# Expert stage of a hybrid encoder step: from 128 gathered and 416 dense tokens to 160 gathered and 384 dense

## The chip, the cores and the metric

One core of a Trainium2 chip (trn2) runs the whole step. The metric is the device time of one execution in microseconds. Engines are named as in the profile: PE (TensorE matmul), PEld (its weight loads), DVE (VectorE), ACT (ScalarE), POOL (GpSimd), SP (SyncE, which here only issues DMAs).

## The reference, cut to what matters

544 tokens (512 of a prompt, 32 of a running stream) pass an input projection, stick-breaking attention, an RWKV-7 branch, a mixing and an output projection, and then the expert layer, which is what the change touches:

```python
q = (xf @ w_q).reshape(n, PEER_HEADS, 2, PEER_HALF)
...
best, sel = lax.top_k(cand, PEER_TOPK)
idx = jnp.take_along_axis(cidx, sel, axis=-1).reshape(n, PEER_HEADS * PEER_TOPK)
gate = jax.nn.softmax(best, axis=-1).reshape(n, PEER_HEADS * PEER_TOPK).astype(xn.dtype)
...
u = jnp.take(u_tab, ib, axis=0)
h = jax.nn.gelu(jnp.einsum('nkd,nd->nk', u, xb), approximate=False)
vv = jnp.take(v_tab, ib, axis=0)
return jnp.einsum('nk,nkd->nd', gb * h, vv)
```

Each token picks 8 x 16 = 128 of 16,384 experts. An expert has a row of 2048 floats in u_tab and one in v_tab. The output is the sum of the 128 rows of v, each times gate times gelu(row of u . token). All is float32.

## The kernel before, in words

**Two ways for the expert layer.** For the first TD = 416 tokens the layer is computed densely: all 16,384 experts are multiplied with all tokens, and a matrix of gates, zero except for a token's picks, selects. For the last 128 tokens only the picked rows are fetched: one indirect DMA on POOL's queue (L2016) brings, for pick number s, one row of 8 KB per partition (128 tokens on 128 partitions, so 1 MB), first 128 times from u (turned by the program into rows in u_d beforehand), then 128 times from v. DVE takes the dot product of a u row with its token (L2251, the token in PSUM, the four banks of accs) and adds a v row times its coefficient to Y (L2259, R and Y both in SBUF). R has GBUF = 3 buffers; a gather waits until its buffer has been used.

**Units.** The dense work is made of weight units of 128 x 2048 floats (1 MB) in a double buffer (class Stream, L119). SP loads a unit into raw (L145), ACT rounds it to whi (L150 whole, L164 half), POOL computes wlo = raw - whi (L154, L168), PE multiplies in three terms (product, L227): whi x hi, whi x lo, wlo x hi, so 16 blocks x 3 = 48 matmuls per unit with all TD tokens as columns. A unit of u is 128 experts by all 2048 channels. A unit of v is 256 experts by 1024 channels (v_rows, L242): for each of 8 blocks of 128 channels PE makes 6 matmuls into one PSUM bank, and DVE adds the bank to H (L2241). So there are 128 units of each, 12,288 matmuls with 416 columns, and 1,024 additions to H. Units of the projections instead make 96 matmuls with 272 columns.

**Where the u units run.** 2 run in the second norm, 24 in retrieval (the choice of the picks, L1522), 16 in gate_matrix (L1775) and 2 at the start of experts (L1886); their gelu is stored in pre_d. Retrieval has 8 iterations, one per head, in which DVE finds the picks. gate_matrix has 8 blocks of GB_T = 52 tokens; in each, PE makes 13 groups ("quads") of one-hot products between matmuls of the units, ACT copies them to STG and SP stores them to g_d.

**experts.** FIRST = 22 groups of 256 experts have their u part already; for these only v units run, with H's additions from four banks of accs. chi and clo, the high and low parts of the coefficients (gelu x gate, made by DVE L2224, ACT L2138, DVE L2230), have two slots, so that those of the next group are made while PE multiplies this one. Then the tokens of the gathered part are turned into rows (32 small matmuls, L2093 and L2094, ACT L2185, L2189). In the 42 groups after that two u units (into psS) and two v units (into psR and psS) alternate, and the 256 gathered rows are spread over them by hand: phases (L1914) says how many gathers POOL issues and between which halves of wlo, and rows_of (L2243) where DVE takes the rows between its additions. Each engine runs its own list in order; the semaphores ex_added, ex_coef, gx_done and those of Stream tie them together. At the end Y is turned back (L2110) and added to H, and the last norm runs.

Of the kernel before, what the change touches and what calls it, by code (L numbers as in the profile page):

```python
# [14 lines left out]
P = 128  # L15
# [18 lines left out]
TD = 416  # L34
# [18 lines left out]
GBUF = 3  # L53
# [65 lines left out]
class Stream:  # L119
# [37 lines left out]
    def half(self, t, c, h):  # L157
        return t[:, c % 2, :].rearrange("p (k e n) -> p k e n", k=2, e=2)[:, :, h, :]
# [81 lines left out]
def v_rows(A):  # L240

    return A["v"].rearrange("(g k p) (h n) -> g h p k n", k=2, p=P, h=2)  # L242


def build(nc, A, O):
    ctx = ExitStack()
    with ctx:
# [35 lines left out]
        with ExitStack() as back:  # L283
            sbk = lambda n, s, d=F32: back.enter_context(nc.sbuf_tensor(n, s, d))

            hh, hl = sbk("hh", [P, KB, T], F32R), sbk("hl", [P, KB, T], F32R)
            load_h = lambda a, b: h_d[a:b].rearrange("k p t -> p k t")
# [12 lines left out]
            IDX, GT = sbk("IDX", [P, P], U32), sbk("GT", [P, P])  # L300
            with ExitStack() as picks:
                IT = picks.enter_context(nc.sbuf_tensor("IT", [P, 3, TD], F32))
                iota = picks.enter_context(nc.sbuf_tensor("iota", [P, P], F32))
                retrieval(nc, S, A, W.phase(base["retrieval"]), [A["u"][TAIL], A["u"][TAIL + 1]], acc, psS, psR, hh, hl, IT, iota, IDX, GT, pre_d)
                gate_matrix(nc, S, A, W.phase(base["gates"]), [A["u"][PRE - 2], A["u"][PRE - 1]], acc, psS, psR, hh, hl, IT, iota, g_d, pre_d)
            H = sbk("H", [P, KB, T])
            experts(nc, S, A, W.phase(base["experts"]), accs, psS, psR, H, load_h, hh, hl, IDX, GT, g_d, pre_d, u_d)
# [1214 lines left out]
def retrieval(nc, S, A, W, ahead, acc, psS, psR, hh, hl, IT, iota, IDX, GT, pre_d):  # L1522
# [4 lines left out]
    with ExitStack() as ctx:  # L1527
# [11 lines left out]
        GEL = sb("tk_GEL", [P, 2, TD])  # L1539
        N = 4  # L1540
        OFF = [0, P, 2 * P, TD, 3 * P]
# [9 lines left out]
        def _(sp):  # L1551
# [27 lines left out]
            blocks(AFTER // 2 - 1, True)  # L1579
            for u in range(2):  # L1580
                sp.wait_ge(S[f"tk_kept{u}"], 16 * (TAIL // 2))

# [11 lines left out]
        def _(pe):  # L1594
# [31 lines left out]
            for j, t in enumerate((0, 1, 2, 4)):  # L1626
# [8 lines left out]
        def _(act):  # L1635
# [37 lines left out]
            for j, t in enumerate((0, 1, 2, 4)):  # L1673
# [6 lines left out]
        def _(dve):  # L1680
# [79 lines left out]
            picked = lambda a: OUT[:, a, 3].rearrange("p h k -> p (h k)")  # L1760
            dve.scalar_tensor_tensor(IDX[:, :], picked(0), float(NK), picked(1), ALU.mult, ALU.add)
            dve.wait_ge(S["tk_gate"], 4)
            dve.tensor_copy(GT[:, :], picked(2)).then_inc(S["tk_gather"], 1)
            dve.wait_ge(S["tk_gather"], 1)


GB_T = 52
# [7 lines left out]
def gate_matrix(nc, S, A, W, ahead, acc, psS, psR, hh, hl, IT, iota, g_d, pre_d):  # L1775
# [3 lines left out]
    with ExitStack() as ctx:  # L1779
# [5 lines left out]
        STEPS = [2, 2, 3, 2, 3, 2, 3, 2, 3, 2, 3, 2, 3]  # L1785
        ITER = GB_N // 2
        MIDDLE = QUADS // 2
        SLOT = [*range(4)] * 3 + [1]
# [97 lines left out]
def experts(nc, S, A, W, accs, psS, psR, H, load_h, hh, hl, IDX, GT, g_d, pre_d, u_d):  # L1886


    with ExitStack() as ctx:
        sb = lambda n, s, d=F32: ctx.enter_context(nc.sbuf_tensor(n, s, d))  # L1890
        G = sb("Ge", [P, 2, GB_N, 2, GB_T])
        GE = sb("GE", [P, 2, TD])
        chi, clo = sb("chi", [P, 2, 2, TD], F32R), sb("clo", [P, 2, 2, TD], F32R)
        R, Y = sb("R", [P, GBUF, D]), sb("Y", [P, D])
        HD, identr = sb("HD", [P, P]), sb("identr", [P, P], F32R)
        GROUPS = NK // 2
        N = 8
        even, odd = R[:, 0, 0:T], R[:, 0, D // 2:D // 2 + T]
        squares = [R[:, 1, 0:T], R[:, 1, D // 2:D // 2 + T], R[:, 2, 512:512 + T], R[:, 2, 1280:1280 + T]]
        square_at = lambda d: (even, odd)[d] if d < 2 else squares[(d - 2) % 4]  # L1900
        all_ones = R[:, 2, 0:P]
        v_units = v_rows(A)
        block = ctx.enter_context(nc.Block())
        FIRST = PRE // 2
        ITER = (GROUPS - FIRST) // 2 - 1
        C0 = START + 2 * FIRST
        UNITS = C0 + 2 + N * ITER + 6

        u_bank = lambda c: psS[:, c % 2, 0:TD]
        v_banks = [psR[:, 0, 0:TD], psR[:, 1, 0:TD], psS[:, 0, 0:TD]]  # L1910
        v_bank = lambda d, per: v_banks[d % 3] if per == N else accs[:, d % 4, 0:TD]
        early = R[:, 2, 0:2 * TD].rearrange("p (k t) -> p k t", k=2)

        gathers, phases = [], []  # L1914
        dotted = summed = 0
        for j in range(GROUPS - FIRST):
            in_u, in_v = 4, 2 + j % 4 // 3 if j else 0
            nv = min(dotted - summed, 3 if dotted < P else in_u + in_v)
            nu = min(in_u + in_v - nv, P - dotted)
            us, vs = [("u", dotted + n) for n in range(nu)], [("v", summed + n) for n in range(nv)]  # L1920
            order = us[:1] + vs + us[1:]
            phases.append((order[:in_u], order[in_u:], len(gathers)))
            gathers += order
            dotted, summed = dotted + nu, summed + nv
        assert dotted == P and summed == P, (dotted, summed)
# [7 lines left out]
        def _(sp):  # L1933
            def u_unit(c, i, k):
                W.load(sp, row(A["u"], k), c, N, i)

            def v_unit(c, i, group, half, per=N):
                src = v_units[group, half] if isinstance(group, int) else v_units[bass.ds(group, 1), half].rearrange("g p k n -> (g p) k n")
                W.load(sp, src, c, per, i)

            def gates(group, slot, count):
                sp.wait_ge(S["ex_coef"], count)
                src = g_d.rearrange("b p n t -> p b n t")
                if isinstance(group, int):
                    a = src[:, :, 2 * group:2 * group + 2, :]
                else:
                    a = src[:, :, bass.ds(2 * group, 2), :]
# [8 lines left out]
            for h in range(2):  # L1956
                v_unit(2 + h, 0, 0, h)
# [415 lines left out]
```

## Time and profile before

| | |
|---|---|
| Median of 3 runs | 4850.69 us (4841.92 to 4850.75) |
| The profiled execution | 4852.76 us, its span 4850.9 us |
| PE busy | 4605.5 us (95%) |
| POOL busy | 2246.2 us (46%) |
| DVE busy | 2973.9 us (61%) |
| Mean granted TensorE clock | 0.98 |
| gate_matrix, experts | from about 2563 us, from about 2825 us to the end |

Matmuls are pipelined: a matmul of 0.35 us begins while the one before it is still counted, so the distance between two starts is what a matmul costs, not its duration. A line at L236 is the helper product, so stages are told apart by the tiles. Spans on POOL are rough. Windows of the stretch from 3400 to 4700 us lie inside the 42 groups.

### The profile page before, as it was taken

How to read it: one execution, taken by the hardware profiler on the slowest of the kernel's cores; microseconds unless marked ns; L12 is line 12 of the kernel's file. 1: busy time of each engine (PE TensorE's matmuls, PEld its weight loads, DVE VectorE, ACT ScalarE, POOL GpSimd, SP SyncE). 2: the span in 40 equal slices, each digit the busy share in tenths (PEclk: the TensorE clock that was granted, in tenths of full speed). 3: DMA queues.
4: the chain of work that ended last, by engine and by line, in shares of the span. 5: the costliest groups of instructions: out<-in, count | busy, mean ns of one | idle time of the engine just before them, and what ended most of it. 6: DMA issues, size and time to landing. Idle time of an engine off the chain costs nothing. (4 is left out here: it accounts for less than half of the span.)

```text
span 4850.9 us, 88014 instructions
## 1 busy us (share of the span) xinstructions
PE 4605.5 (95%) x33924; PEld 4418.6 (91%) x33924; DVE 2973.9 (61%) x4755; ACT 1398.0 (29%) x1813; POOL 2246.2 (46%) x865
## 2 busy tenths in 40 slices
PE   6999899999999898979999989999999999999997
PEld 5999888888888798979998989999999999999997
DVE  4333355555555432259977946657777777777777
ACT  3333322222222221122223323333332333233332
POOL 1332221222222232334443245547787777778876
PEclk8999999999999999999999999999999999999999
DMA  6999733334443477942233465448888888888884
GB/s 237 345 367 359 284 129 133 122 127 134 134 134 133 154 221 267 313 148 95 104 124 150 182 248 161 158 148 305 296 304 307 304 292 303 310 299 297 307 292 170
DMA packets 344256, 1078.68 MB, mean 222 GB/s; under 512 B 99457, under 2 KB 154113, under 8 KB 264961
## 3 DMA queue, kind: packets, MB, share of 16 engines
q1 hardware_dynamic: 292272, 784.66, 46.7%
q0 software_dynamic: 36864, 268.45, 14.8%
q10 hardware_dynamic: 14928, 22.84, 1.3%
q8 instruction: 142, 2.33, 0.2%
q14 instruction: 50, 0.40, 0.0%
HBM read 877.69 MB, written 198.14 MB: 222 GB/s over the span
## 5 line engine op out<-in xcount | busy, mean ns | idle before, releaser
L154 POOL TENSOR_TENSOR wlo<-raw,whi 128x2048 fp32r<-128x2048 f32 x174 | 803.1, 4616 | 2020.7 <-ACT whi L150 1725.2
L168 POOL TENSOR_TENSOR wlo<-raw,whi 128x1024 fp32r<-128x1024 f32 x424 | 1040.6, 2455 | 498.9 <-ACT whi L164 492.2
L164 ACT ACTIVATE whi<-raw 128x1024 fp32r<-128x1024 f32 x424 | 449.7, 1061 | 983.9 <-PE psR L236 367.0
L236 PE MATMUL accs<-xh,whi 128*128 128x272 f32 x2624 | 581.8, 303 | 56.0 <-POOL wlo L154 26.6
L2259 DVE SCALAR_TENSOR_TENSOR Y<-R,HD,Y 128x2048 f32<-128x2048 f32 x127 | 441.4, 3476 | 233.6 <-DMA R<-in_v,IDX 229.2
L236 PE MATMUL accs<-xh,wlo 128*128 128x272 f32 x2624 | 547.5, 290 | 0.0
L236 PE MATMUL accs<-xl,whi 128*128 128x272 f32 x2624 | 546.5, 290 | 0.0
L236 PE MATMUL accs<-hh,whi 128*128 128x272 f32 (+1 forms) x1696 | 465.3, 323 | 47.2 <-POOL wlo L154 22.4
L236 PEld LDWEIGHTS accs<-xh,whi 128*128 128x128 f32 x2624 | 416.8, 190 | 86.0 <-issue 39.4
L236 PE MATMUL psS<-hh,wlo 128*128 128x416 f32 x1344 | 474.1, 353 | 0.0
L236 PE MATMUL psS<-hh,whi 128*128 128x416 f32 x1344 | 471.0, 350 | 0.0
L236 PE MATMUL psS<-hl,whi 128*128 128x416 f32 x1344 | 469.3, 349 | 0.0
L236 PE MATMUL accs<-hh,wlo 128*128 128x272 f32 (+1 forms) x1696 | 451.2, 315 | 0.0
L236 PE MATMUL accs<-hl,whi 128*128 128x272 f32 (+1 forms) x1696 | 449.4, 314 | 0.0
L236 PEld LDWEIGHTS accs<-xl,whi 128*128 128x128 f32 x2624 | 417.2, 191 | 0.0
L236 PEld LDWEIGHTS accs<-xh,wlo 128*128 128x128 f32 x2624 | 415.4, 191 | 0.0
L150 ACT ACTIVATE whi<-raw 128x2048 fp32r<-128x2048 f32 x174 | 332.4, 1911 | 142.1 <-DMA raw<-in_w_out 73.1
L236 PEld LDWEIGHTS accs<-hh,whi 128*128 128x128 f32 x1696 | 291.2, 190 | 58.8 <-POOL wlo L154 24.4
L210 DVE STREAM_TRANSPOSE at_UO<-at_UI 128x2048 f32<-128x2048 f32 x64 | 147.9, 2312 | 310.2 <-DMA at_UI<-in_u 310.0
L236 PE MATMUL psR<-chi,whi 128*128 128x416 f32 x924 | 330.2, 357 | 0.7 <-DVE H L2241 0.5
L236 PE MATMUL psR<-chi,wlo 128*128 128x416 f32 x924 | 326.1, 353 | 0.0
L236 PE MATMUL psR<-clo,whi 128*128 128x416 f32 x924 | 323.7, 350 | 0.0
(406 smaller groups left out, 9313.0 us busy)
## 6 DMA issues: line engine op xcount, KB each, us to landing
raw<-in_u SPq DMA_DIRECT2D x128, 1024.0 KB, 4.9
raw<-in_v SPq DMA_DIRECT2D x128, 1024.0 KB, 5.7
raw<-in_w_in SPq DMA_DIRECT2D x82, 1024.0 KB, 8.5
at_UI<-in_u SPq DMA_DIRECT2D x64, 1024.0 KB, 9.2
u_d<-at_UO SPq DMA_DIRECT2D x256, 256.0 KB, 6.5
g_d<-STG SPq DMA_DIRECT2D x8, 3328.0 KB, 10.3
Ge<-g_d SPq DMA_DIRECT2D x64, 416.0 KB, 10.8
wo_UI<-in_u SPq DMA_DIRECT2D x24, 1024.0 KB, 8.4
```

The costliest lines, as they stand in the source:

```text
L150: act.activation(self.hi[:, c % 2, :], self.raw[:, c % 2, :], ACT.Copy).then_inc(self.hi_done, 2)
L154: pool.tensor_tensor(self.lo[:, c % 2, :], self.raw[:, c % 2, :], self.hi[:, c % 2, :].bitcast(F32), ALU.subtract).then_inc(self.split_don ...
L164: act.activation(self.half(self.hi, c, h), self.half(self.raw, c, h), ACT.Copy).then_inc(self.hi_done, 1)
L168: pool.tensor_tensor(self.half(self.lo, c, h), self.half(self.raw, c, h), self.half(self.hi, c, h).bitcast(F32), ALU.subtract).then_inc(se ...
L210: dve.transpose(self.uo(b).rearrange("p (e k j) -> p e k j", e=4, j=32), self.ui(a).rearrange("p (k e j) -> p e k j", e=4, j=32)).then_inc ...
L236: mm = pe.matmul(out, w(k), x(k, n), start=a, stop=z)
L2259: dve.scalar_tensor_tensor(Y[:, :], r, HD[:, x:x + 1], Y[:, :], ALU.mult, ALU.add).then_inc(S["gx_done"], 1)
```

## The change

The dense part takes TD = 384 tokens and 160 are gathered. The last 128 tokens ("A") are gathered as before. The 32 others ("B") are laid out four picks at a time: partition 32r + t holds pick 32r + n of token t, so 32 gathers bring all their 128 rows of each table. That makes 160 gathers from u and 160 from v. The picks of B are moved to their partitions by 8 small DMAs at the end of retrieval; their tokens are turned by 32 more small matmuls at the start of experts and stand in SBUF (XB), where those of A still stand in PSUM (accs). The sums of B's four partitions per token are made at the end by 16 matmuls with sel. YA, YB and XB lie in columns of H, hh and hl that the dense part doesn't use any more.

A unit of v now holds 512 experts by 512 channels: 4 blocks of 128 channels with 12 matmuls each, so still 128 units with 48 matmuls, but 512 additions to H instead of 1,024. A row of v in a unit is read in pieces of 2 KB instead of 4 KB. Groups have 512 experts: FIRST = 11 without u units, then 21 with four u units and four v units. chi and clo have one slot for the four key blocks instead of two for two. The v units use the four banks psR and psS in turn, and accs is kept for the tokens of A from the start. Gathers run in the first phase too (2 in group 0, 4 in each of the next ten), 13 or 14 in each of the twenty groups after that, 7 in the last, with four buffers. POOL issues a gather by a written time table (when, issue). gate_matrix has GB_T = 48, 12 quads per block.

```diff
-TD = 416
+TD = 384
...
-GBUF = 3
+GBUF = 4
...
-    return A["v"].rearrange("(g k p) (h n) -> g h p k n", k=2, p=P, h=2)
+    return A["v"].rearrange("(g k p) (h n) -> g h p k n", k=4, p=P, h=4)
...
+                sp.dma_start(IDXB[part, :], IB[:, cols]).then_inc(S["few_moved"], 16)
+                sp.dma_start(GTB[part, :], OUT[0:DEC, 2, 4].rearrange("p h k -> p (h k)")[:, cols]).then_inc(S["few_moved"], 16)
...
-GB_T = 52
+GB_T = 48
...
+        G, GE = sb("Ge", [P, GB_N, 4, GB_T]), sb("GE", [P, 4, TD])
+        CHI, CLO = sb("chi", [P, 4, TD], F32R), sb("clo", [P, 3, TD], F32R)
...
+        YA, YB, XB = H[:, :, spare], over[0][:, :, spare], over[1][:, :, spare]
...
+        chi = lambda k: CHI[:, k, :]
+        clo = lambda k: CLO[:, k, :] if k < 3 else hh[:, 0:TD // DEC, tail]
...
+        SUPERS, FIRST, U = NK // 4, PRE // 4, 8
...
+        u_bank = lambda n: psS[:, n % 2, 0:TD]
+        v_bank = lambda dd: (psR, psS)[dd // 2][:, dd % 2, 0:TD]
...
+        seq = [x for n in range(DEC) for x in [("A", 4 * n + m) for m in range(4)] + [("B", n)]]
...
+                  "long": [(0, 0.1), (0, 0.4), (0, 0.7), (1, 0.3), (1, 0.7), (2, 0.3), (2, 0.7), (3, 0.3),
+                           (4, 0.4), (5, 0.1), (5, 0.8), (6, 0.2), (6, 0.8), (7, 0.2)]}
...
+        issue = [max(3.0, when[n - GBUF] + 0.4 if n >= GBUF else 0.0) for n in range(len(gathers))]
...
+            def first_groups(i, begin):
+                for h in range(begin, 4):
+                    v_unit(START + h, i, i, h, 4)
+                sp.wait_ge(S["ex_prod"], 4 * i + 4)
+                gates(i + 1)
+                for k in range(4):
+                    sp.wait_ge(S["ex_coef"], 4 * i + k + 1)
+                    kept(i + 1, k)
...
+            for c in range(2, UNITS):
+                for h in range(2):
+                    gather(c - 1.4 + 0.5 * h)
...
+            def v_first(c, i, s, per):
+                for half in range(2):
+                    W.ready(pe, c, per, i, half)
+                for k in range(4):
+                    pe.wait_ge(S["ex_coef"], 4 * s + (k + 1 if per == 4 else max(k + 1, 3)))
+                    for dd in range(3):
+                        if k == 0:
+                            pe.wait_ge(S["ex_added"], 16 * s + dd + 1)
+                            if per == 4:
+                                pe.wait_ge(S["ex_xb_read"], dd + 1)
+                        mm = channel(c, dd, [k])
+                        if k == 3:
+                            done(mm, dd)
+                pe.wait_ge(S["ex_added"], 16 * s + 4)
+                if per == 4:
+                    pe.wait_ge(S["ex_xb_read"], 4)
+                done(channel(c, 3, [*range(4)]), 3)
...
+            def v_products(c, i, s, h, per):
+                for dd in range(4):
+                    if dd % 2 == 0:
+                        W.ready(pe, c, per, i, dd // 2)
+                    pe.wait_ge(S["ex_added"], 16 * s + 4 * h + dd + 1)
+                    done(channel(c, dd, [*range(4)]), dd)
...
+            pe.wait_ge(S["ex_early"], START)
+            for k in range(KB):
+                out = (psR, psS)[k // 8][:, k // 4 % 2, k % 4 * P:(k % 4 + 1) * P]
+                pe.matmul(out[0:DEC], hh[:, k, TD:TD + DEC], identr[:, :], start=k % 4 == 0, stop=False, skip_group_check=True)
+                mm = pe.matmul(out[0:DEC], hl[:, k, TD:TD + DEC], identr[:, :], start=False, stop=True, skip_group_check=True)
...
+            def u_units(i, s):
+                for k in range(4):
+                    if k < 2:
+                        pe.wait_ge(S["ex_added"], 16 * s + 3 + k)
+                    else:
+                        pe.wait_ge(S["ex_coef"], 4 * s + k - 1)
+                    u_products(C0 + k, i, u_bank(k), U)
...
+                mm = pe.matmul(accs[:, 0, DEC * k:DEC * k + DEC], YB[:, k, :], sel[:, :], start=k == 0, stop=k == KB - 1,
+                               skip_group_check=True)
...
+            for s in range(SUPERS):
+                if s >= FIRST:
+                    for k in range(4):
+                        c = C0 + U * (s - FIRST) + k
+                        hi(c + 2, 0)
+                        W.wait_used(act, c)
+                        act.activation(u_bank(k), u_bank(k), ACT.Gelu).then_inc(S["ex_gelu"], 1)
+                        hi(c + 2, 1)
+                        coef_hi(4 * s + k)
+                for h in range(4):
+                    c = v_of(s, h)
+                    hi(c + 2, 0)
+                    if h == 3 and s + 1 < FIRST:
+                        W.wait_used(act, c)
+                        for k in range(4):
+                            coef_hi(4 * s + 4 + k)
+                    hi(c + 2, 1)
+                    if h == (3 if s == 0 else 2 if s < FIRST else 0):
+                        gather_gelu(s)
...
+                        if which == "A":
+                            dve.tensor_tensor_reduce(r, r, accs.rearrange("p b n -> p (b n)"), 1.0, 0.0, ALU.mult, ALU.add,
+                                                     coef).then_inc(S["gx_done"], 1)
+                        else:
+                            dve.tensor_tensor_reduce(wide, wide, XB, 1.0, 0.0, ALU.mult, ALU.add, coef).then_inc(S["gx_done"], 1)
...
+            for s in range(FIRST):
+                ahead = s + 1 < FIRST
+                for h in range(4):
+                    if h == 2 and s == 0:
+                        dve.wait_ge(S["ex_turned"], 8)
+                        dve.wait_ge(S["few_moved"], 256)
+                    rows(1 if s or h >= 2 else 0)
+                    for dd in range(3):
+                        add(s, 4 * h + dd)
+                    if h == 3 and ahead:
+                        for k in range(4):
+                            coef_lo(4 * s + 4 + k)
+                    add(s, 4 * h + 3)
+                    if h == 1 and ahead:
+                        for k in range(4):
+                            scale(4 * s + 4 + k)
...
+            for s in range(FIRST, SUPERS - 1):
+                rows(3 if kinds[s] == "long" else 2)
+                for k in range(2):
+                    scale(4 * s + k)
+                    rows(1)
+                    coef_lo(4 * s + k)
+                    rows(1)
+                scale(4 * s + 2)
+                rows(1)
+                coef_lo(4 * s + 2)
+                scale(4 * s + 3)
+                coef_lo(4 * s + 3)
+                rows(1)
+                for d in range(4):
+                    add(s, d)
+                for h in (1, 2):
+                    rows(1)
+                    for dd in range(4):
+                        if dd == 2:
+                            rows(1)
+                        add(s, 4 * h + dd)
+                rows(1)
+                for dd in range(4):
+                    add(s, 12 + dd)
```

## Rows read from the trace of the kernel before

**Rows 1.** The page: span, busy time, and GB/s in 40 slices

```profile
span 4850.9 us, 88014 instructions
...
PE 4605.5 (95%) x33924; PEld 4418.6 (91%) x33924; DVE 2973.9 (61%) x4755; ACT 1398.0 (29%) x1813; POOL 2246.2 (46%) x865
...
GB/s 237 345 367 359 284 129 133 122 127 134 134 134 133 154 221 267 313 148 95 104 124 150 182 248 161 158 148 305 296 304 307 304 292 303 310 299 297 307 292 170
```

**Rows 2.** Windows: stretch, busy us per engine (instructions), granted clock, DMA share, GB/s

```profile
200.00:300.00 100.00, 99.65 (x756) 95.64 (x756) 31.39 (x24) 33.34 (x37) 32.03 (x7) 1.00 0.99 356
2139.00:2539.00 400.00, 400.00 (x2631) 392.98 (x2630) 337.22 (x1218) 96.96 (x106) 168.90 (x37) 1.00 0.30 106
2563.00:2818.00 255.00, 243.09 (x1600) 239.08 (x1600) 232.67 (x520) 96.07 (x136) 70.64 (x15) 0.98 0.44 172
2900.00:3200.00 300.00, 300.00 (x1576) 293.11 (x1575) 184.53 (x327) 98.81 (x129) 158.01 (x66) 1.00 0.52 165
3400.00:4700.00 1300.00, 1296.41 (x6744) 1255.03 (x6743) 990.23 (x1033) 391.31 (x569) 1023.08 (x499) 1.00 0.83 302
```

**Rows 3.** Timeline of PE: start, duration, form, at 272 columns and at 416

```profile
299.79 0.42 PE L236 MATMUL accs<-xh,wlo 128*128 128x272 f32 x2
...
301.81 0.41 PE L236 MATMUL accs<-xl,whi 128*128 128x272 f32 x2
...
3899.77 0.35 PE L236 MATMUL psR<-clo,whi 128*128 128x416 f32 x1
...
3901.09 0.35 PE L236 MATMUL psR<-chi,wlo 128*128 128x416 f32 x1
```

**Rows 4.** Groups of instructions, 3400 to 4700 us: busy us, mean ns, idle before

```profile
L168 POOL TENSOR_TENSOR wlo<-raw,whi 128x1024 fp32r<-128x1024 f32 x281 | 684.7, 2437 | 243.0 <-ACT whi L164 237.3
...
L2259 DVE SCALAR_TENSOR_TENSOR Y<-R,HD,Y 128x2048 f32<-128x2048 f32 x107 | 375.8, 3512 | 203.4 <-DMA R<-in_v,IDX 199.8
...
L2251 DVE CUSTOM_DVE_ANT_0 R<-R,accs 128x2048 f32<-128x2048 f32 x113 | 257.3, 2277 | 0.0
L2241 DVE TENSOR_TENSOR H<-psR,H 128x416 f32<-128x416 f32 x385 | 218.6, 584 | 75.6 <-PE psR L236 74.8
...
L2016 POOL DMA_INDIRECT R<-u_d,IDX x113 | 173.1, 1531 | 17.6 <-issue 12.7
L2016 POOL DMA_INDIRECT R<-in_v,IDX x105 | 165.4, 1575 | 16.7 <-issue 4.6
...
L2138 ACT ACTIVATE chi<-psS 128x416 fp32r<-128x416 f32 x70 | 36.3, 519 | 54.1 <-DVE psS L2224 54.1
```

**Rows 5.** Waits of PE: total us, times, longest

```profile
PE accs L236 <- DVE H L2241: 8.6, 1, 8.6
PE psS L236 <- DVE clo L2230: 7.8, 12, 2.6
```

**Rows 6.** Window just after that longest wait, columns as in rows 2

```profile
2858.50:2865.00 6.50, 6.16 (x19) 5.89 (x20) 2.96 (x6) 1.06 (x1) 2.37 (x1) 0.53 0.72 238
```

**Rows 7.** Timeline of PE: first and last of the 32 turning matmuls

```profile
3268.26 0.22 PE L2093 MATMUL accs<-identr,hh 128*128 128x128 f32 x1
...
3271.67 0.28 PE L2094 MATMUL accs<-identr,hl 128*128 128x128 f32 x1
```

**Rows 8.** Timeline of SP's queue at the end of retrieval

```profile
2555.95 0.35 SPq L1576 DMA_DIRECT2D pre_d<-tk_GEL  x1
```

**Rows 9.** Tile R: duration ns min/median/max, first and last start

```profile
L2016 POOL DMA_INDIRECT R<-u_d,IDX x128: 937/952/2830, 2888.4 to 4677.8; - x128
...
L2259 DVE SCALAR_TENSOR_TENSOR Y<-R,HD,Y x127: 2340/3451/4458, 3298.0 to 4790.8; 128x2048 f32<-128x2048 f32 x127
```

**Rows 10.** Timelines of DVE and of POOL near 4105 us

```profile
4102.20 7.57 DVE L2259 SCALAR_TENSOR_TENSOR Y<-R,HD,Y 128x2048 f32<-128x2048 f32 x2
...
4107.76 2.83 POOL L2016 DMA_INDIRECT R<-in_v,IDX  x1
```

**Rows 11.** DMA issues: KB each, median us to landing

```profile
R<-in_v,IDX POOLq DMA_INDIRECT x128, 7.4
```

More of the change, by code:

```diff
@@ L1672, in _ @@
             blocks(AFTER // 2 - 1)
-            for j, t in enumerate((0, 1, 2, 4)):
+            for j, t in enumerate((0, 1, 2)):
                 n = rows(t)
@@ new lines, in experts @@
+        dotted = summed = 0
+        kinds = []
+        for s in range(SUPERS):
+            left = 2 * PICKS - len(gathers) - len(places["last"])
+            kind = ("start" if s == 0 else "first" if s < FIRST else "last" if s == SUPERS - 1 else
+                    "long" if left > len(places["short"]) * (SUPERS - 1 - s) else "short")
+            kinds.append(kind)
+            n = len(places[kind])
+            nv = min(dotted - summed, n if dotted == PICKS else n // 2)
+            nu = min(n - nv, PICKS - dotted)
+            dots.append((dotted, nu))
+            gathers += [("u", dotted + m) for m in range(nu)] + [("v", summed + m) for m in range(nv)]
+            c = START + 4 * s if s < FIRST else C0 + U * (s - FIRST)
+            when += [c + at + f for at, f in places[kind]][:nu + nv]
@@ new lines, in add, with rows @@
+            def add(s, d):
+                h, dd = d // 4, d % 4
+                if s == 0 and dd == 0:
+                    dve.wait_ge(S[f"ex_h{h}"], 16)
+                if dd % 2:
+                    W.wait_used(dve, v_of(s, h), half=dd // 2)
+                else:
+                    dve.wait_ge(S["ex_v"], 8 * s + 2 * h + dd // 2 + 1)
+                dve.tensor_tensor(H[:, d, 0:TD], v_bank(dd), H[:, d, 0:TD], ALU.add).then_inc(S["ex_added"], 1)
+            taken = [0]
+            def rows(count):
+                for n in range(taken[0], min(taken[0] + count, len(gathers))):
+                    kind, m = gathers[n]
+                    which, x = seq[m]
+                    r, coef = R[:, n % GBUF, :], HD[:, m:m + 1]
+                    wide = r.rearrange("p (k n) -> p k n", n=P)
@@ L2297, in _ @@
+            s = SUPERS - 1
+            rows(2)
+            for k in range(3):
+                scale(4 * s + k)
+                rows(1)
+                coef_lo(4 * s + k)
+                rows(1 if k < 2 else 0)
+            scale(4 * s + 3)
+            coef_lo(4 * s + 3)
+            assert taken[0] == len(gathers)
+            for d in range(4):
+                add(s, d)
             dve.wait_ge(S["ex_yt"], 1)
+            dve.wait_ge(S["ex_rest"], 16)
             for b in range(4):
-                h = H[:, 4 * b:4 * b + 4, TD:T]
```

510 lines of the change are left out of this document (203 added, 307 removed).

## The prediction

> **What bounds the kernel now.** I read the page first, for which engine is full, then the windows by stage, then PE's timeline for the price of one matmul, then the waits and groups of the loop. The page says that PE is busy 95% of the span [rows 1], but its matmuls overlap, so I take the distance between two starts instead. From 3899.77 to 3901.09 lie 7 starts, so 188.6 ns for 416 columns; from 299.79 to 301.81 lie 16, so 126.2 ns for 272 [rows 3]. In the loop of the 42 groups 6744 matmuls take 1300 us, 192.8 ns each [rows 2]. So 6744 x 188.6 = 1271.9 us is pure matmul, and 28 us, 2.2%, is stall: 0.8 us in each of its 35 groups. Before the loop the first phase shows 300 - 1576 x 0.1886 = 2.8 us of stall in 300 [rows 2]. PE, at full clock, is the limit nearly everywhere in the expert part; the longest single wait there is 8.6 us, once [rows 5]. Behind it DVE is busy 76% and POOL 79% of the loop, and the DMA engines 83% at 302 GB/s [rows 2]. These three set how far a faster PE can run.
>
> **Fewer columns.** All 12,288 dense matmuls lose 32 columns. The two prices give (188.6 - 126.2) / 144 = 0.433 ns a column, 13.9 ns for 32; 32 columns at 2.4 GHz, the clock granted in both stretches [rows 2], are 13.3. I take 13.6: 167 us, of which 166 count, as the 96 matmuls under the second norm follow DVE. The ends are 163 and 171. That weight loads don't set the distance is seen at 272 columns, where one passes every 126 ns. In retrieval PE has no gap in 400 us while DVE works 337 [rows 2], so its 24 units gain too.
>
> **gate_matrix.** A block takes 255 / 8 = 31.9 us [rows 2], of which 96 dense matmuls are 18.1; the other 13.8 are 13 quads, 1.06 each. One quad less in 8 blocks: -8.5 (ends -5 and -12; DVE, 91% busy, loses a thirteenth too).
>
> **End of retrieval.** The eight DMAs for B's picks and gates stand in SP's queue behind the last store, issued at 2555.95 in 0.35 us [rows 8]. At that price they add 2.8 us before the last landing, and the dropped fourth turning of picks gives some back: +2 (0 to +4).
>
> **Start of experts.** Before, PE waits 8.6 us once [rows 5] because the second group's gelu is loaded late behind other DMAs; then the clock is at its lower level, 0.53 for 6.5 us, with 19 matmuls where some 34 fit [rows 2, 6]: about 3 us. Then come 3.6 us for the 32 turning matmuls [rows 7]. After, H is loaded first, all four gelu blocks of group 0 come early, and PE has the turning to do while the coefficients are made: 32 matmuls for A and 32 for B, 7.2 us, and about 2 us until ACT has freed psR. So 15.2 becomes 9.2: -6 (ends -12 and +5, if one DMA is late again).
>
> **First phase.** chi now has one slot. At each of ten group ends ACT waits for the last matmul, then makes chi(0), then DVE clo(0), then PE starts: 0.35 - 0.19 of drain, 0.52, 0.58 and about 0.2 of semaphores, 1.4 us [rows 3, 4], with clo at the price of an addition to H. That is 14 us (9 to 25), less 2 for half as many ordinary joints: +12. The loads of g_d and pre_d for the next group are issued early in the group and used at its middle, about 17 us in, where a gather takes 7.4 [rows 11]; they are covered.
>
> **Loop.** Eight units now take 384 x 175.0 = 67.2 us, where two groups took 74.0. Ordinary stall: 0.8 us per four units stays as a rate, 1.6 per group (between 0.8, if it goes with the group ends, and 5, below). So nothing is added or taken. The 2.6 us wait for clo before the first group [rows 5] goes: -3.
>
> DVE loses half of the additions (16 x 0.5 per group) and gains rows: 13.5 per group instead of 12.4 per pair of groups. 6.8 v rows at 3.51, 5.4 A dots and 1.4 B dots, 24 short operations at 0.48: 24 + 12.3 + 4.9 + 11.5 = 53 of 67 us [rows 4]. In the half with the v units it is tighter: 6 v rows and 16 additions are 29 of 33.6 us, and PE's four banks give it some 3 us of play. POOL's time is priced among the rivals.
>
> **The B dots** read R and XB, both in SBUF; the A dots read PSUM and take 2.277 us whatever POOL does, v rows, with both operands in SBUF, from 2.34 to 4.46 [rows 4, 9]. I price a B dot like a v row, 3.5 us, bounds 2.3 and 4.5. The Trainium skill, SBUF — State Buffer, section "Who interferes with whom", says that a DVE instruction with two SBUF inputs contends with a GpSimd instruction that reads SBUF, and that whoever comes second is blocked for the whole instruction. The spread of the v rows agrees with it. The same section infers that descriptor generation is not held up by such a DVE instruction; here a gather at 4107.76 takes 2.83 us under a v row [rows 10] and the median is 0.95 [rows 9], so the rows speak against that, and I go by them.
>
> **End.** 16 matmuls with sel and one more addition: +2.5 (1 to 6). The loop's last group takes seven v rows before PE needs them, about 4 us apart, in time.
>
> **Sum.** -166 - 8.5 + 2 - 6 + 12 - 3 + 2.5 = -167, against the profiled execution's 4852.8, 4686; that execution lies 2 us above the median, so 4684.
>
> **Rival 1, POOL becomes the bound (slower than before).** A group needs 16 halves of wlo at 2.44, 13.6 gathers and about 2 us of issue. Gathers average 1.55 now, that is 32% at 2.83 and the rest at 0.95 [rows 4, 9]. If the slow ones are those that meet a two-SBUF operation of DVE, present 29% of the time now (375.8 of 1300) and 42% after (8.2 x 3.5 of 67), the mean goes to 1.75: 39 + 24 + 2 = 65 of 67.2, nearly full, where it was 60 of 74. POOL is in order: a gather that waits for its buffer holds the next wlo. If every gather meets DVE, 39 + 38.5 + 2 = 79.5 per group, 10.7 over the 68.8 of my forecast, in 21 groups 225: 4909. It becomes the bound from a mean of 1.95 us, and the kernel slower than before from 2.65. Against: the measured 0.95 whenever POOL is free, and the time table that sets gathers between halves. Chance 0.10, with anything else that loses as much.
>
> **Rival 2, PE gains the columns, but DMA, POOL or DVE give part back.** Per group 8 units, 13.5 rows (1.049 MB each) and 0.79 MB of gates are 23.3 MB, in 67.2 us 347 GB/s. The loop shows 302 at share 0.83, which scales to 364 at a full share; the fullest slice of the page has 367, and the densest window 356 at 0.99 [rows 1, 2]. So it fits with 5% to spare, if v's pieces of 2 KB cost no more than those of 4. If this mix stops at 320 GB/s, a group takes 72.8, 4 more than 68.8: +84, 4768. The same 1 to 5 us per group come if POOL's 65 us and DVE's late rows make PE wait: in the loop DVE already waits 200 us for 105 v rows [rows 4]. This case gives 4700 to 4790. The Trainium skill, DMA: Bandwidth & Descriptors, section "Where 436 GB/s comes from", puts HBM's share of a core at about 358 GB/s. By it the 347 would just pass; the slice of 367 shows that the figure is no hard ceiling here. Chance 0.27.
>
> **Chances.** My forecast, PE bound at 175 ns with the old rate of stalls, 4650 to 4700: 0.60. Rival 2: 0.27. Slower: 0.10. Within 0.2%, about what a measurement of this kernel can tell from no change: 0.02. The last 0.01 is a gain beyond 4650. The range has to take in rival 2: 4650 to 4790 leaves out about 0.14. Faster: 0.60 + 0.27 + 0.01 = 0.88.
>
> **What would show it.** Starts 175 ns apart in the loop and a group period of 68 to 69 us prove the main term; a period over 70 with PE waiting for wlo is POOL, with PE waiting for additions to H and DVE waiting for R is DMA. Gathers from 1.7 us in the mean, and B dots at about 3.5 us, confirm the port. gate_matrix should last 235 us, ten waits of about 1.4 us should stand in the first phase, and no 8.6 us wait at its start. The forecast is wrong if the distance between matmuls stays near 188, if POOL's share of the loop reaches 98%, or if the GB/s of the loop stays under 330.

## The result, and the profile after

The changed kernel takes 4793.37 us in the median of 5 runs (4786.91 to 4809.33), against 4850.69 before: ratio 0.9893, interval 0.9871 to 0.9916. The gain is 57 us where 167 were forecast. Its profiled execution took 4788.95 us, 64 less than that of before. These are the head of the page and its groups:

```profile
span 4787.2 us, 86830 instructions
PE 4449.2 (93%) x33921; PEld 4303.0 (90%) x33921; DVE 2972.1 (62%) x4301; ACT 1360.4 (28%) x1786; POOL 2434.3 (51%) x929
```

PE's share fell from 95 to 93%, while POOL's rose from 46 to 51%. The question is in which stage the 103 us between 4686 and 4789 went. I took the starts of the first and last matmuls of each stage from both traces, and set the change beside what the steps of the prediction make of it (0.65 us per weight unit, and the term of that stage):

| stage | before | after | change | forecast |
|---|---|---|---|---|
| start to retrieval | 2146.3 | 2150.2 | +4.0 | 0 |
| retrieval | 408.9 | 393.4 | -15.5 | -15.7 |
| its end, to gate_matrix | 9.7 | 10.0 | +0.3 | +2 |
| gate_matrix | 259.7 | 233.1 | -26.6 | -18.9 |
| start of experts and first phase | 434.6 | 425.1 | -9.5 | -24 |
| loop with u units | 1564.5 | 1545.7 | -18.8 | -113 |
| end | 27.1 | 29.5 | +2.4 | +2.5 |

The first line is no effect of the change: other kernels here, with the same work there, show 2142 to 2159. Nearly the whole miss, 94 us, is in the loop: 4.5 us in each of its 21 groups. The windows by stage (gate_matrix, first phase, two of the loop), columns as in [rows 2]:

```profile
2545.00:2785.00 240.00, 226.19 (x1539) 222.49 (x1539) 220.96 (x480) 94.90 (x132) 78.22 (x17) 0.98 0.47 183
2850.00:3150.00 300.00, 281.97 (x1605) 279.36 (x1604) 203.94 (x252) 92.42 (x132) 223.01 (x102) 0.99 0.82 282
3250.00:4550.00 1300.00, 1227.51 (x6812) 1211.99 (x6811) 995.91 (x796) 381.81 (x573) 1129.34 (x525) 0.98 0.88 319
3300.00:4600.00 1300.00, 1227.33 (x6814) 1212.40 (x6812) 1005.19 (x790) 384.08 (x572) 1138.25 (x525) 0.98 0.88 320
```

The loop makes 6812 matmuls in 1300 us, 190.8 ns each, where [rows 2] had 192.8 with 32 more columns. Yet the usual distance between two starts is 174 ns. So PE has its new price and loses it in pauses. PE's waits in the stretch from 3300 to 4600, and below them four lines of the waits of DVE and POOL there:

```profile
PE psS L236 <- DVE H L2270: 53.5, 25, 3.3
PE psR L236 <- DVE H L2270: 10.5, 18, 2.3
PE psR L236 <- POOL wlo L168: 5.9, 1, 5.9
```

```profile
DVE psS L2249 <- ACT psS L2211: 244.2, 69, 7.3
POOL wlo L168 <- ACT whi L164: 110.4, 77, 3.2
DVE H L2270 <- PE psS L236: 16.8, 18, 1.5
DVE R L2284 <- DMA R<-u_d,IDX: 8.0, 7, 2.7
```

PE waits 64 us for additions to H. Most of it (46 us, once in each of 17 groups) comes where the next group's u units need psS; the rest are shorter waits inside the half with v units. DVE waits only 8 us for rows in R, and is idle 244 us in the half with u units. So the data are there, and DVE is late in one half of the group and has nothing to do in the other. The groups of the same stretch show what made it late, against [rows 4]:

```profile
L168 POOL TENSOR_TENSOR wlo<-raw,whi 128x1024 fp32r<-128x1024 f32 x285 | 709.3, 2497 | 113.5 <-ACT whi L164 110.4
L2295 DVE SCALAR_TENSOR_TENSOR H<-R,HD,H 128x2048 f32<-128x2048 f32 x94 | 405.5, 4314 | 0.0
L2284 DVE CUSTOM_DVE_ANT_0 R<-R,accs 128x2048 f32<-128x2048 f32 x97 | 219.8, 2276 | 8.3 <-DMA R<-u_d,IDX 8.0
L2287 DVE CUSTOM_DVE_ANT_1 R<-R,over_hl 128x2048 f32<-128x2048 f32 x25 | 81.7, 3267 | 1.1 <-DMA R<-u_d,IDXB 1.1
L2039 POOL DMA_INDIRECT R<-u_d,IDX x95 | 182.6, 1922 | 21.5 <-issue 16.1 <-DVE HD L2287 4.9
L2039 POOL DMA_INDIRECT R<-in_v,IDX x97 | 162.5, 1676 | 17.4 <-issue 13.6
```

A v row takes 4.31 us where it took 3.51; the dots with a PSUM operand stay at 2.28. A u gather takes 1.92 us instead of 1.53. How a v row comes to 4.3 is seen in the timelines of DVE and POOL at the end of one v half:

```profile
4069.69 6.91 DVE L2295 SCALAR_TENSOR_TENSOR H<-R,HD,H 128x2048 f32<-128x2048 f32 x1
4077.45 2.33 DVE L2295 SCALAR_TENSOR_TENSOR H<-R,HD,H 128x2048 f32<-128x2048 f32 x1
4079.72 1.01 DVE L2270 TENSOR_TENSOR H<-psS,H 128x384 f32<-128x384 f32 x2
4080.65 6.88 DVE L2295 SCALAR_TENSOR_TENSOR H<-R,HD,H 128x2048 f32<-128x2048 f32 x1
4087.45 1.01 DVE L2270 TENSOR_TENSOR H<-psR,H 128x384 f32<-128x384 f32 x2
4088.38 1.00 DVE L2270 TENSOR_TENSOR H<-psS,H 128x384 f32<-128x384 f32 x2
```

```profile
4069.67 4.77 POOL L168 TENSOR_TENSOR wlo<-raw,whi 128x1024 fp32r<-128x1024 f32 x2
4074.60 2.83 POOL L2039 DMA_INDIRECT R<-u_d,IDX  x1 [0.16 <-issue]
4077.73 2.87 POOL L2039 DMA_INDIRECT R<-u_d,IDX  x1 [0.30 <-issue]
4080.62 4.75 POOL L168 TENSOR_TENSOR wlo<-raw,whi 128x1024 fp32r<-128x1024 f32 x2
```

The row at 4077.45 comes ahead of POOL and takes 2.33 us; the gather beside it takes 2.87 instead of 0.95. The rows at 4069.69 and 4080.65 begin 0.02 and 0.03 us after POOL has begun two halves of wlo back to back: 4.6 us of waiting and 2.33 of work. The other rows fit: reckoned from the end of the last half of wlo that stood ahead, each of the kernel's 158 v rows takes 2.33 us, within 0.25; one that waits for a whole half takes 4.55, for two 6.9. Behind the rows shown stand the last additions of the group, and behind those PE, whose timeline shows the pause and what follows it:

```profile
4085.38 0.34 PE L236 MATMUL psS<-chi,wlo 128*128 128x384 f32 x1
4089.06 0.68 PE L236 MATMUL psS<-hh,whi 128*128 128x384 f32 x1 [3.34 <-DVE H L2270]
4089.54 0.52 PE L236 MATMUL psS<-hl,whi 128*128 128x384 f32 x1
4089.86 0.52 PE L236 MATMUL psS<-hh,wlo 128*128 128x384 f32 x1
```

```profile
4089.00:4091.00 2.00, 1.94 (x6) 1.95 (x7) 2.00 (x2) 0.00 (x0) 1.98 (x2) 0.50 1.00 401
4095.00:4097.00 2.00, 2.00 (x13) 2.00 (x12) 0.00 (x0) 0.76 (x1) 0.47 (x1) 1.00 0.68 119
```

After the pause the matmuls start 0.32 us apart at a granted clock of 0.50, 1.2 GHz; some microseconds later it is 1.00 again. From 3300 to 4600 some 160 matmuls start 0.32 us apart and some 40 others 0.28, which costs about 26 us beside the 64 of waiting. Of the 110 v rows into tile H from 3200 to 4700, 30 took 6.8 us or more; in the kernel before, none took over 4.5. The long rows stand where PE is near: in the half with v units the six rows of a group take 4.49 us each in the mean, and with the 16 additions that is 34.9 us of DVE's work beside 33.4 of matmuls (192 at 174 ns).

### The profile page after: what moved, and what is told of

The parts are those of the page before. It is cut to its first block and busy times, and to the rows that moved or that the text cites. A ratio compares the mean times of both kernels' runs of the same rounds, so it can differ in the third digit from the quotient of the medians.

```text
span 4787.2 us, 86830 instructions
## 1 busy us (share of the span) xinstructions
PE 4449.2 (93%) x33921; PEld 4303.0 (90%) x33921; DVE 2972.1 (62%) x4301; ACT 1360.4 (28%) x1786; POOL 2434.3 (51%) x929
## 3 DMA queue, kind: packets, MB, share of 16 engines
q0 software_dynamic: 46080, 335.56, 18.8%
q8 instruction: 142, 2.33, 0.2%
## 5 line engine op out<-in xcount | busy, mean ns | idle before, releaser
L168 POOL TENSOR_TENSOR wlo<-raw,whi 128x1024 fp32r<-128x1024 f32 x424 | 1067.2, 2526 | 262.0 <-ACT whi L164 258.1
L236 PE MATMUL psS<-hh,whi 128*128 128x384 f32 x1600 | 556.2, 348 | 57.1 <-DVE H L2270 52.4
L2295 DVE SCALAR_TENSOR_TENSOR H<-R,HD,H 128x2048 f32<-128x2048 f32 x127 | 528.6, 4162 | 0.1
L236 PE MATMUL psS<-hl,whi 128*128 128x384 f32 x1344 | 465.3, 346 | 0.0
L236 PE MATMUL psS<-hh,wlo 128*128 128x384 f32 x1344 | 463.8, 345 | 0.0
L236 PE MATMUL psR<-chi,whi 128*128 128x384 f32 x1024 | 348.2, 340 | 41.0 <-DVE clo L2260 19.5
L236 PEld LDWEIGHTS psS<-hh,whi 128*128 128x128 f32 x1600 | 310.7, 194 | 64.4 <-issue 56.9
L236 PE MATMUL psS<-chi,whi 128*128 128x384 f32 x1024 | 343.9, 336 | 9.7 <-DVE H L2270 7.7
L236 PE MATMUL psR<-chi,wlo 128*128 128x384 f32 x1024 | 344.2, 336 | 0.0
```

The costliest lines, as they stand in the source:

```text
L168: pool.tensor_tensor(self.half(self.lo, c, h), self.half(self.raw, c, h), self.half(self.hi, c, h).bitcast(F32), ALU.subtract).then_inc(se ...
L236: mm = pe.matmul(out, w(k), x(k, n), start=a, stop=z)
L2295: dve.scalar_tensor_tensor(y, wide, coef, y, ALU.mult, ALU.add).then_inc(S["gx_done"], 1)
```

## The experiments

**The theory** after this: DVE's operations with two SBUF operands and POOL's work exclude each other; with POOL fuller, its halves of wlo come in pairs, a v row that comes second waits for both, and the additions behind it make PE wait. **The rivals:** DVE is simply too long in the v half, whatever POOL does; the DMA engines can't carry the new rate; the B dots, which also read two SBUF operands, are the cause; POOL itself is full. In all kernels below the windows are those of 3250 to 4550, to be held against the 6812 matmuls, POOL 1129 and 319 GB/s above. In the diffs accs stands for the view of that tile in the shape of the row.

**1. v rows that add PSUM.** The second operand becomes accs, so this kernel leaves out the sum of the rows so far.

```diff
-dve.scalar_tensor_tensor(y, wide, coef, y, ...)
+dve.scalar_tensor_tensor(y, wide, coef, accs, ...)
```

> Every v row adds the tokens in PSUM (accs) instead of the sum so far, so the gathered half of the result is wrong, but the instruction has one operand in SBUF instead of two. Theory (lock): DVE's v rows with two SBUF operands wait for POOL's wlo halves and POOL's gathers wait for them; then v rows take 2.3 us each, gathers 0.95, PE's waits for additions to H fall from about 70 us to under 10, a group lasts 69 us instead of 72.3, and the time is 4710 to 4730. Rival (DMA): the rows land too late at 320 GB/s; then the group stays above 72 and DVE waits for R instead, time within 15 us of 4793. Rival (POOL is simply full): some gain through shorter gathers, as with the lock; the next run tells these apart.

4658.68 us in one run, beside 4844.31 for the kernel before. Window and groups of the loop:

```profile
3250.00:4550.00 1300.00, 1294.63 (x7416) 1293.04 (x7415) 834.14 (x857) 415.31 (x619) 1026.43 (x571) 1.00 0.93 348
L2295 DVE SCALAR_TENSOR_TENSOR H<-R,HD,accs 128x2048 f32<-128x2048 f32 x107 | 250.2, 2338 | 1.2 <-DMA R<-in_v,IDX 1.0
L2039 POOL DMA_INDIRECT R<-in_v,IDX x108 | 104.4, 967 | 19.3 <-issue 13.3
```

A single operand's place gives back over 130 us, more than the 63 to 83 that were expected: those had the waits for H go, and not the lower clock behind them. The v rows take 2.34, the gathers 0.97, a matmul 175.3 ns with all pauses. The DMA engines carry 348 GB/s meanwhile, so DMA was not what held the loop, and the forecast 175.0 ns could be had with this very order of work. From its first to its last matmul the loop lasts 1419 us; the forecast comes to 1452, the changed kernel to 1546.

**2. The same, made long.** Before each row of the loop DVE copies 1536 floats from PSUM, so that a row takes its old time without the exclusion.

```diff
+dve.tensor_copy(GE, accs[:, 0:4 * TD])
 dve.scalar_tensor_tensor(y, wide, coef, accs, ...)
```

> As the run before, but from the first group with u units on each v row is preceded by a copy of 1536 floats from PSUM, so that DVE spends about 4.0 us per v row, nearly the 4.3 us of the changed kernel, without touching the port that it shares with POOL. Theory (lock, through POOL and through the bunching of waits up to 6.9 us): gathers at 0.95, and most of the gain stays, 4715 to 4745. Rival (the mean length of DVE's work in the v half alone makes PE wait): 6 rows of 4.0 and 16 additions are 32 of 33.4 us, so PE waits nearly as much as in the changed kernel, 4770 to 4795.

```profile
3250.00:4550.00 1300.00, 1278.54 (x7271) 1270.58 (x7270) 1022.07 (x971) 408.03 (x612) 1008.38 (x564) 1.00 0.92 342
PE psS L236 <- DVE H L2270: 9.9, 18, 0.9
```

4693.88 us in one run, 21 less than the best expected. A row with its copy takes 2.34 + 1.75 = 4.08 us and DVE is as busy as in the changed kernel (1022 and 996 of 1300), but only 35 of the 135 us are lost again, and PE waits some 10 us for additions to H instead of 64. So it is not DVE's total work that holds the loop. The test stops short in one place: in the half with v units the locked rows take 4.49 us in the mean, 34.9 with the additions, and the pairs 4.08, which makes 32.5, still under the 33.4 that the matmuls need. How much of the loss comes from the length of that half, how much from where its long rows stand and how much from slower gathers is therefore not shown. That all three come from the exclusion is, by experiment 1.

**3 and 4. Other orders of the rows in the loop.** One kernel lets rows of u and v alternate from the first group with u units, the other takes the v rows first. In the alternating one a group's v rows are spread over both halves. In both, ACT's gelu of the dots (gather_gelu) moves from the first v unit of a group to the last.

```diff
-gathers += us + vs
+gathers += us + vs if s < FIRST else [x for m in range(max(nu, nv)) for x in us[m:m + 1] + vs[m:m + 1]]
```

```diff
-gathers += us + vs
+gathers += us + vs if s < FIRST else vs + us
```

> Same work, other order: from the first group with u units on, u and v rows alternate, so the half with the v units has 3 v rows instead of 6 and the half with the u units has 3 to 4. The gelu of a group's dots moves to its last unit. Theory (DVE is late in the v half, where v rows stand before additions that PE waits for): the half has 3 x 4.3 + 3 x 2.4 + 16 x 0.5 = 28 of 33.4 us, in the u half DVE has had 244 us of idle time in 1300; PE's waits for H fall by two thirds and the time is 4720 to 4750. Rival (POOL full or DMA): total work unchanged, time within 15 us of 4793.

> As the run before, but all v rows of a group come first and the dots last, so that the half with the v units has one row with two SBUF operands at most besides B's dots. Theory: fewest waits for additions to H, but seven v rows of 4.3 us plus eight short operations, 34 us, fill the u half of 33.4 us and make clo late for u units 2 and 3; 4720 to 4770, near the alternating order. Rival (POOL or DMA): within 15 us of 4793.

Both came out as expected. Alternating: 4733.84 us, ratio 0.9763 (0.9746 to 0.9779); v first: 4767.1, 0.9837 (0.9821 to 0.9853), with PE waiting 35 us for wlo and 26 for clo, since the rows now stand between DVE and the coefficients. The alternating kernel's loop:

```profile
3250.00:4550.00 1300.00, 1263.01 (x7144) 1253.61 (x7143) 1021.93 (x833) 403.15 (x601) 1203.79 (x547) 0.99 0.90 334
L2298 DVE SCALAR_TENSOR_TENSOR H<-R,HD,H 128x2048 f32<-128x2048 f32 x95 | 384.2, 4044 | 9.4 <-DMA R<-in_v,IDX 9.4
PE psR L236 <- POOL wlo L168: 22.7, 12, 3.4
PE psS L236 <- DVE H L2273: 6.0, 4, 1.9
```

The rows are still locked (4.04 us), but the waits for H fall from 64 to about 11 us, as DVE's load now lies in the half where it was idle. What comes in their place is POOL, busy 1204 of 1300 us. The two limits stand one behind the other.

**5 and 6. A gap between two halves of wlo.** POOL waits for its own last half to be written, so a waiting row can come between. Alone, and with the alternating order.

```diff
 W.split_lo_half(pool, c, h)
+pool.wait_ge(W.split_done, 2 * (W.base + c) + 5 + h)
```

> The changed kernel, and POOL waits after each wlo half for that half to be done before it issues the next instruction. Theory: a v row that waits for the port waits through two wlo halves when they run back to back (rows of 6.9 us = 2.3 + 4.6); with a gap DVE gets the port after one, the rows of 6.8 us and more vanish, the mean falls from 4.3 to 3.6, and the time from 4793 to 4730 to 4760. Rival (POOL is full, so every wait added there costs): POOL loses 16 x 0.1 us per group, time 4795 to 4830. Rival (no hand-over between two queued instructions is at stake, a row just waits for whatever runs): no change of the row lengths, within 10 us of 4793.

> The alternating order with the gap. Theory: the rest of PE's waits for wlo and H goes, 4690 to 4715. If the gap only helps where v rows are bunched: as the alternating order, 4734. If POOL is full: 4740 to 4760.

4773.99 us, ratio 0.986 (0.9842 to 0.9879), 14 more than the slowest expected, and 4741.83, 0.9789 (0.9772 to 0.9805), where 4690 to 4715 was expected and 4740 to 4760 if POOL is full. In the first kernel's loop:

```profile
L2296 DVE SCALAR_TENSOR_TENSOR H<-R,HD,H 128x2048 f32<-128x2048 f32 x92 | 332.5, 3614 | 1.1 <-DMA R<-in_v,IDX 1.1
PE psR L236 <- POOL wlo L168: 48.9, 18, 6.8
PE psS L236 <- DVE H L2271: 5.3, 7, 1.6
DVE R L2285 <- DMA R<-u_d,IDX: 102.0, 64, 5.0
```

The mechanism is right: v rows fall to 3.61 us, none is over 5.0, and the waits for H are all but gone. The forecasts of gain were not: what a row waits less, POOL loses, and PE waits for wlo instead (49 us, and 14 more with psS). With the alternating order the gap gains nothing, 4742 against 4734, and PE waits 50.6 us for wlo; in the two traces the loop itself lasts 1506 us with it and 1488 without. Both expectations erred in the same place: they took POOL's time for free.

**7 and 8. The start of experts mended**, alone and with both parts before. coef_hi comes after the last early gelu instead of the first, and the first gather later (its rows are taken in the last unit of group 0).

```diff
-if c == 0:
+if c == START - 1:
     for n in range(4):
         coef_hi(n)
...
-issue = [max(3.0, ...
+issue = [max(4.1, ...
```

> The changed kernel with two edits at the start of the expert stage: ACT makes the first four chi after the second early gelu instead of before it (PE waits 4.6 us for that gelu), and the first gathers, which make POOL wait for the small DMAs and hold the next wlo, are issued 1.1 units later and taken in the last unit of group 0 (PE waits 2.3 and 7.2 us in group 0 and at its end). Theory: both waits vanish but for about 2 us, 4779 to 4786. Rival (DMAs of H, gelu blocks and gates are what is late): under 3 us gained, 4790 to 4797.

> Alternating order, gap and mended start together. Theory: the gains add, 4680 to 4705, which reaches the forecast of 4684 within 1%. If the gap does not help: 4722 to 4730.

4789.6 us, ratio 0.99 (0.9879 to 0.992), where 4779 to 4786 was expected: not told apart from the 4793 of the change. In the trace the four waits at the start (4.3, 0.8, 2.0, 6.8 us) became two of 3.4 and 4.7; some 6 us, too little for a sum of this spread. The last of them, at the end of group 0, is the exclusion once more. In the changed kernel:

```profile
2811.60 1.49 DVE L2260 TENSOR_TENSOR clo<-GE,chi 128x384 fp32r<-128x384 f32 x3
2857.50 8.22 DVE L2260 TENSOR_TENSOR clo<-GE,chi 128x384 fp32r<-128x384 f32 x3 [3.48 <-ACT chi L2166]
2857.01 4.65 POOL L168 TENSOR_TENSOR wlo<-raw,whi 128x1024 fp32r<-128x1024 f32 x2
```

In the first phase clo reads GE and chi, both in SBUF. Beside an idle POOL the three take 1.49 us. Here the first waits for these two halves of wlo and the third for one more, and they take 8.22. All three parts together: 4733.93, 0.9784 (0.9765 to 0.9803), some 30 us over what was expected if the gains add, since the gap gives nothing once POOL is full.

**9. B dots that read PSUM.**

```diff
-dve.tensor_tensor_reduce(wide, wide, XB, ...)
+dve.tensor_tensor_reduce(wide, wide, accs, ...)
```

> The changed kernel with one edit: the 32 dot products of B take the tokens in PSUM (those of A) as second operand instead of XB in SBUF, so B's part of the result is wrong. Theory (lock): B's dots fall from 3.2 us to 2.3, and the gathers under them to 0.95; they lie in the u half, where DVE is idle, so PE gains little: 4775 to 4793. Rival (B's dots are what makes POOL late and so bunches the wlo halves): 4750 or less.

4801.24 us in one run (4775 to 4793 was expected), no gain. The B dots, 3.27 us in the mean in the changed kernel, take 2.28 here, but they stand in the half where DVE has time: PE waits 53.4 and 9.5 us for H as before. They are not the cause.

**10. The kernel before, with v rows that add accs** in place of Y.

> The kernel before, with v rows that add the tokens in PSUM instead of Y, so the gathered part is wrong. Theory: the lock is there too (rows 3.5 us, a third of the gathers at 2.83) but covered, since its v half has two groups' worth of slack and PE waits for H only briefly; v rows 2.3, gathers 0.95, time 4825 to 4845, at most 20 us better. Rival (the lock already costs the kernel before as much as the changed one, so that it explains none of the difference): 4720 to 4790.

4836.74 us in one run beside 4844.44. Its groups in the loop:

```profile
L2259 DVE SCALAR_TENSOR_TENSOR Y<-R,HD,accs 128x2048 f32<-128x2048 f32 x104 | 244.0, 2346 | 144.1 <-DMA R<-in_v,IDX 140.6
L2016 POOL DMA_INDIRECT R<-in_v,IDX x105 | 100.3, 955 | 17.1 <-issue 5.7 <-DVE HD L2251 0.6
```

The exclusion was there before: without it rows fall from 3.51 to 2.35 and gathers from 1.58 to 0.96 [rows 4]. But it cost only some 8 us (9 in the loop, from trace to trace), for a group of 37 us left both engines enough room. The change did not bring the mechanism; it took away its cover.

**11. Alternating rows, and DVE makes 3 of a group's 16 halves of wlo.**

```diff
-W.split_lo_half(pool, c, h)
+if (c, h) in by_dve:
+    pool.wait_ge(W.split_done, 2 * (W.base + c) + 5 + h)
+else:
+    W.split_lo_half(pool, c, h)
...
+W.split_lo_half(dve, c, 1)
```

> The alternating order, and DVE makes the second wlo half of three of a group's eight units (1.1 us each by the price of a two-operand subtraction of 1024 floats, where POOL takes 2.4). Theory (in the alternating order PE waits as much for POOL's wlo as for H, since POOL is 93% busy): POOL falls to 85%, 4705 to 4728. Rival (DVE has no room, or the hand-over between the two engines costs more than it saves): 4735 to 4765.

```profile
3250.00:4550.00 1300.00, 1277.14 (x7260) 1271.44 (x7260) 1025.75 (x897) 408.56 (x612) 1053.86 (x504) 0.99 0.91 340
L2309 DVE SCALAR_TENSOR_TENSOR H<-R,HD,H 128x2048 f32<-128x2048 f32 x101 | 347.6, 3441 | 9.3 <-DMA R<-in_v,IDX 9.2
PE psR L236 <- POOL wlo L168: 17.6, 8, 4.7
PE psS L236 <- DVE H L2278: 1.7, 2, 1.1
```

4692.27 us, ratio 0.9683 (0.9667 to 0.9699): 101 us below the change and 152 below the 4844.44 measured with it for the kernel before. It is the fastest of those that compute the whole layer, and lies 8 us from the forecast. POOL falls to 1054 of 1300 us and v rows to 3.44 us, since fewer of POOL's halves are there to wait for. It gained 13 us more than the best that was expected. While DVE makes a half, it can't be locked out by POOL making the same; I read the surplus so, without a run that shows it.

**12. All gathers in the loop**, none in the first phase, alternating.

```diff
-places = {"start": [(2, 0.5), (3, 0.5)], "first": [(0, 0.4), (1, 0.4), (2, 0.5), (3, 0.5)],
+places = {"start": [], "first": [],
```

(two gathers more in each of the twenty groups after, and two more places where DVE takes a row)

> The alternating order with one part of the change undone: no row is gathered in the first eleven groups, 313 of the 320 are in the twenty groups with u units, 15 or 16 each instead of 13 or 14. Theory (the port is the scarce thing in the loop): 2.1 more rows per group add 1.05 v rows and 2.1 gathers to an engine pair with nothing to spare, 2 to 5 us per group, 4775 to 4835, while the first phase gets no faster than its ten waits allow. Rival (rows in the first phase cost there what they save in the loop): within 10 us of the alternating order, 4734.

4805.94 us, ratio 0.9918 (0.9899 to 0.9937), 72 more than with the gathers spread, as expected. In its loop 6736 matmuls take 1300 us and PE waits 54.2 us for additions. From trace to trace the first phase with the start of experts gets 4 us shorter (424.9 to 421.2) and the loop 81 us longer (1488 to 1569): a row costs next to nothing in the first phase and much in the loop.

## Why the prediction was right and wrong

The 4793 us lie 3 us above the stated range of 4650 to 4790, and 109 above the forecast in it.

**Right:** the main term. The distance between two starts went to 174 ns (forecast 175.0), and retrieval lost 15.5 us of 15.7. Experiment 1 shows it in the whole loop. The first phase: its waits for the only slot of chi, with one of 6.8 us that belongs to the start,

```profile
PE psR L236 <- DVE clo L2260: 19.5, 10, 6.8
```

are 12.7 us for nine, 1.4 each, as worked out. The end: +2.4 for +2.5. B dots: 3.27 us, under the 3.5 taken. That gathers are slowed by a v row: in the trace before, all 70 slow gathers of 218 overlap a v row and none of the others does.

**Wrong: the loop, "so nothing is added or taken".** The step that failed is the one below it: "6 v rows and 16 additions are 29 of 33.6 us, and PE's four banks give it some 3 us of play". It carried over 3.51 us per row from a kernel in which POOL had 60 us of work in 74. With 64 in 72.9 the row takes 4.31, and in the half with v units 4.49, so 6 x 4.49 + 16 x 0.5 = 34.9 of 33.6 us: the half is over-full. The sum of the half seems to count more than a single long row. In 10 of the 18 groups the last row ahead of the additions took 6.9 us and PE waited 3.3; in the other 8 the last two took 4.5 to 4.6 each, and PE waited 2.0 and, a little earlier, 1.0. The same text had the port, the bounds of 2.34 to 4.46 and POOL at 65 of 67 us; it priced POOL and DVE each by itself, and never asked what POOL's filling does to DVE. The Trainium skill, SBUF — State Buffer, section "Who interferes with whom", calls the port pair that DVE and GpSimd share an exclusive lock. A DVE instruction with two SBUF inputs contends there with a GpSimd instruction that reads SBUF, and whoever issues first has the pair for the whole instruction, while the other is fully blocked. The timeline agrees (a v row of 2.33 us takes 6.91), and adds that two such instructions in a row can pass before a waiting one is served. What the step missed cost 4.5 us per group. The 64 us of waiting for H and 26 of lower clock in some 18 groups are 5 us each, against the 1.6 of stall that the forecast had in all.

**Rival 2** named the right outcome, part given back "if POOL's 65 us and DVE's late rows make PE wait", at 1 to 5 us per group; 4.5 lie inside. The other half of that rival, a mix that stops at 320 GB/s, is refuted: 319 was what PE asked for, and 348 were carried as soon as it asked. One of the three signs of being wrong came too: the loop's GB/s stayed under 330. It told of requests that came late, and not of a bandwidth that ended. The sign set for this rival in the prediction (PE waits for H and DVE for R) came true only in its first half, and that told the two apart. **Rival 1**, POOL as the bound, didn't come about by itself (POOL 1129 of 1300 us), but it is the next limit once DVE's is gone, as experiments 3, 6 and 8 show. That the change doesn't lose against before was right, and so was the sign.

**Start of experts: mis-sized.** Forecast 15.2 us to 9.2. In the trace it is 31.2 us from the first matmul of experts to the first one with chi. Two u units are 16.8 of them, which leaves 14.4 for the turning, the waits and the lower clock, and waits of 2.0 and 6.8 us follow in group 0. The forecast saw the turning. It didn't see that ACT makes four coef_hi ahead of the second early gelu (PE waits 4.3 us), and these stand behind DVE, which is idle 34 us until the gelu blocks have landed, at 2809.7. Nor did it see that POOL's first gather, held until B's picks have been moved, stands ahead of a half of wlo (2.0 us), that clo, with both operands in SBUF, can be locked out too (6.8 us), and that the granted clock is 0.50 from 2812 to 2821 and from 2860 to 2866. The step named each part that moved, but not what was queued behind it on ACT, DVE and POOL. With the first phase, that is 14.5 us of the miss.

**gate_matrix: under-sized.** -26.6 for -18.9: without the columns, 16.2 us for eight quads, beyond even the end of -12. The quad was priced by what it takes of PE, 1.06 us. But DVE is busy 91% of the stage before [rows 2] and 92% after (221 of 240), and falls from some 237 to 215 us in it (those shares of 259.7 and 233.1). So the stage seems to go by DVE's work per quad; no run here tested that.

## What to carry to other kernels

When PE gets faster, every engine beside it gets fuller, and the durations of its neighbours' instructions are no constants: an operation that shares a port has a price that depends on how full the other engine is, so it must be priced at the new fill, and in the half of the loop where it stands: a v row was 3.51 us before, 4.31 after, and 4.49 in the half that PE waits for. Look at idle time by half of the loop, not by its mean: DVE was 77% busy here and late all the same, and moving the rows to the half where it was idle gave 60 us. Then ask which limit stands right behind; a remedy that takes its time from an engine that is nearly full (the gap on POOL) gives nothing, and one that takes work away from it (three halves to DVE) gave the forecast back.

## What was not expected of the hardware

A v row that became ready 0.02 us after POOL's half did not get its turn between two halves: it took 6.91 us, 2.33 and both halves. A wait of POOL on its own result between them let it in (no row over 5.0 us). With an operand in PSUM the same operation took 2.34 us in every case, and gathers 0.97 beside it. And from 3300 to 4600, 8 of the 9 pauses of 3.3 us on PE and 5 of the 8 of 2.0 us were followed by matmuls 0.32 us apart at a granted clock of 0.50 for some microseconds, so that the pauses cost some four tenths more than they last (26 us to 64 here).
